# Final projection of a two-layer encoder: five token tiles summed over heads 0 to 5 beside the last head's inversion and recurrence

## What is computed

```
def deltanet_mixer(hn, w_in, conv_w, a_log, dt_bias, out_norm, w_out):
    proj = hn @ w_in                                   # q, k, v, gate, beta, decay
    ...                                                # short conv, silu, l2 norms
    o_fwd = gated_delta_chunked(q, k, v, g[:, :, 0], beta[:, :, 0])
    o_bwd = flip(gated_delta_chunked(flip(q), flip(k), flip(v), ...))
    o = o_fwd + o_bwd
    o = o * lax.rsqrt(jnp.mean(o * o, axis=-1, keepdims=True) + EPS) * out_norm
    o = (o.reshape(b, s, B_VW) * jax.nn.silu(gate)).astype(hn.dtype)
    return o @ w_out                                   # the final projection

x = x + deltanet_mixer(...)                            # residual x1
return rms_norm(x, final_norm)
```

## Time and profile before

| quantity | value |
|---|---|
| median of three executions | 1497.5 us |
| the profiled execution's own time | 1498.05 us |
| its span in the trace | 1496.3 us |
| PE busy | 1378.8 us (92%) |
| PE weight loads busy | 1010.7 us (68%) |
| DVE busy | 785.8 us (53%) |
| ACT busy | 704.0 us (47%) |
| GpSimd busy | 248.8 us (17%) |
| mean granted TensorE clock | 0.961 of full |
| HBM read, written | 61.04 MB, 12.12 MB |

### The profile page before, as it was taken

How to read it: one execution, slowest core, us unless ns; L and a number is a source line. 1 busy time by engine, 2 the same in 40 slices (tenths; PEclk the granted TensorE clock), 3 DMA queues, 4 the chain that set the end, 5 groups by cost and what they waited for, 6 DMA issues and landing times.

```text
span 1496.3 us, 25718 instructions
## 1 busy us (share of the span) xinstructions
PE 1378.8 (92%) x9981; PEld 1010.7 (68%) x9981; DVE 785.8 (53%) x2200; ACT 704.0 (47%) x1869; POOL 248.8 (17%) x190
## 2 busy tenths in 40 slices
PE   5999999999999987799989899999898999977998
PEld 4866666666444456677778778878787787864443
DVE  6244545444344228665665684666655846552232
ACT  6155554555454234363573654644726546462111
POOL 8111111110011313212121221120212211200000
PEclk9999999999999999899999999999999999988999
DMA  5101000011211111010110210101102001015041
GB/s 175 43 28 29 29 28 30 28 57 57 85 57 57 57 73 42 16 43 30 44 43 16 71 29 16 57 29 44 43 16 72 25 21 43 1 55 214 0 141 56
DMA packets 18455, 74.81 MB, mean 50 GB/s; under 512 B 2848, under 2 KB 3104, under 8 KB 16800
## 3 DMA queue, kind: packets, MB, share of 16 engines
q1 hardware_dynamic: 18336, 73.18, 14.3%
HBM read 61.04 MB, written 12.12 MB: 49 GB/s over the span
## 4 chain that ended last, share of the span: by engine, by line
PE 70%; DVE 16%; ACT 7%; issue 3%; DMA 2%; POOL 1%; SPq 0%; DVEq 0%; ACTq 0%; POOLq 0%
PE bank L1570 16%; PE bank L1691 12%; PE bank L1642 8%; PE bank L1671 7%; DVE arena L1314 4%; PE bank L1597 3%; DVE arena L1354 3%; PE bank L1623 3%; PE bank L1608 3%; PE bank L1825 2%; PE bank L1839 2%; PE bank L1842 2%; PE bank L1750 2%; DVE arena L1487 1%; PE bank L1724 1%
## 5 line engine op out<-in xcount | busy, mean ns | idle before, releaser
L1691 PE MATMUL bank<-hn_hi,w_hi 128*128 128x512 f32 x512 | 227.4, 444 | 0.0
L1691 PE MATMUL bank<-hn_hi,w_lo 128*128 128x512 f32 x512 | 206.8, 404 | 0.0
L1691 PE MATMUL bank<-hn_lo,w_hi 128*128 128x512 f32 x512 | 206.0, 402 | 0.0
L1570 PE MATMUL bank<-hn_hi,w_hi 128*128 128x512 f32 x320 | 139.7, 437 | 0.5 <-ACT arena L944 0.2
L1570 PE MATMUL bank<-hn_hi,w_lo 128*128 128x512 f32 x320 | 125.9, 393 | 0.0
L1570 PE MATMUL bank<-hn_lo,w_hi 128*128 128x512 f32 x320 | 125.8, 393 | 0.0
L1671 PE MATMUL bank<-arena 128*128 128x512 f32 x256 | 114.3, 600 | 10.3 <-DMA arena<-oT_scratch 9.1
L1642 PE MATMUL bank<-arena 128*128 128x512 f32 x256 | 120.1, 600 | 0.0
L876 POOL TENSOR_TENSOR w_lo<-arena,w_hi 128x1024 fp32r<-128x1024 f32 x30 | 74.3, 2476 | 266.2 <-ACT w_hi L1038 266.2
L1691 PEld LDWEIGHTS bank<-hn_hi,w_lo 128*128 128x128 f32 x512 | 99.5, 194 | 22.8
L1691 PEld LDWEIGHTS bank<-hn_hi,w_hi 128*128 128x128 f32 x512 | 100.1, 196 | 17.2
(11 more groups left out here) (227 smaller groups left out, 2655.4 us busy)
## 6 DMA issues: line engine op xcount, KB each, us to landing
arena<-in_w SPq DMA_DIRECT2D x52, 512.0 KB, 3.5
arena<-in_x SPq DMA_DIRECT2D x16, 512.0 KB, 4.4
arena<-gc_scratch SPq DMA_DIRECT2D x8, 1024.0 KB, 4.5
x_scratch<-arena SPq DMA_DIRECT2D x8, 512.0 KB, 2.6
arena<-in_wout SPq DMA_DIRECT2D x1, 4096.0 KB, 13.5
arena<-x_scratch SPq DMA_DIRECT2D x8, 512.0 KB, 4.2
out<-arena SPq DMA_DIRECT2D x8, 512.0 KB, 2.9
oT_scratch<-arena SPq DMA_DIRECT2D x7, 512.0 KB, 5.0
```

The costliest lines, as they stand in the source:

```text
L1570: ins = te.matmul(bank[r % 2][:], wp[:, tile % 2, k], hp[:, k, hf * HALF:(hf + 1) * HALF], start=(k == 0 and m == 0), stop=(k == KT - 1 an ...
L1691: ins = te.matmul(b[:], wp[:, t % 2, k], hp[:, k, hf * HALF:(hf + 1) * HALF], start=(k == 0 and m == 0), stop=(k == KT - 1 and m == 2))
```

## The change

The final projection is cut into three parts. `FIN_EARLY` now counts ten units (token tiles 0 to 4), and `FIN_HEADS = 6` heads.

1. Partial sums: for units 0 to 9, heads 0 to 5, 60 matmuls, as events `("fp", u, j)`. They are put by `fe(n)`: 14 in the last inversion behind stage y5, and two behind each of the recurrence's events 1 to 23. They use banks 0 and 1 in turn.
2. A new DVE event `("part", u)` adds the residual tile to each finished partial sum and keeps it in SBUF (`early_sum`, ten halves, in the space of the layer's weight buffers).
3. The rest: events `("ff", w, j)`, in the order of tiles `FIN_TILES = [5, 0, 1, 2, 6, 3, 4, 7]`. For tiles 0 to 4 only heads 6 and 7 are summed, and DVE adds `early_sum` in place of the residual; tiles 5, 6, 7 are done in full. Between osum and otr stand now the 14 matmuls of tile 5.

The loads follow: SP issues them in an event `("finld",)` of the last inversion, as six pairs of DMAs (one head's weight and one head's output, 512 KB each, counted on three semaphores), one of 1 MB for the weight's heads 6 and 7, and then the first two residual tiles. Head 6's output is loaded later, by a DMA of its own. In the diff, `finld` is SP's part, `part` DVE's and `fp` PE's.

```
-FIN_EARLY = 6
+FIN_EARLY = 10
+FIN_HEADS = 6
...
+        FIN_TILES = [5, 0, 1, 2, 6, 3, 4, 7]
...
+            early = [("fp", 2 * u + hf, j) for u in range(1) for j in range(FIN_HEADS) for hf in range(2)]
+            early = [[e] + ([("part", e[1])] if e[2] == FIN_HEADS - 1 else []) for e in early]
+            for u in range(2, FIN_EARLY):
+                early += [[("fp", u, j)] + ([("part", u)] if j == FIN_HEADS - 1 else []) for j in range(FIN_HEADS)]
+            def fe(n):
+                for items in early[:n]:
+                    ev.extend(items)
+                del early[:n]
...
             def inversion(h):
+                more = f if h < B_HEADS - 1 else fe
...
+                if h == B_HEADS - 1:
+                    put(("finld",))
                 stage("x5", h)
...
-                f(3)
+                more(3)
                 put(("vtr", h, 0), ("vtr", h, 1))
                 stage("x6", h)
-                f(2)
+                more(2)
                 stage("y6", h)
-                f(2)
+                more(2)
...
-            fins = [("fin", u, j) for u in range(2) for j in range(B_HEADS - 1)]
             for n in range(3 * NT):
                 put(("rec", h - 1, n // 3, "abc"[n % 3]))
-                if n >= 10 and fins:
-                    put(fins.pop(0))
+                if n >= 1:
+                    fe(2)
...
             put(("osum", h - 1, 0), ("osum", h - 1, 1), ("osq", h - 1))
-            put(*[("fin", u, j) for u in range(2, FIN_EARLY) for j in range(B_HEADS - 1)])
+            put(*[("ff", w, j) for w in range(2) for j in range(KT - 1)])
             put(("onorm", h - 1), ("otr", h - 1, 0), ("otr", h - 1, 1))
+            put(*[("ff", w, KT - 1) for w in range(2)])
+            for w in range(2, 2 * NT):
+                put(*[("ff", w, j) for j in range(FIN_HEADS if 2 * FIN_TILES[w // 2] < FIN_EARLY else 0, KT)])
...
+                elif e[0] == "finld":
+                    sp.wait_ge(W_full, W_DONE[("proj", NTILES - 1, 1, 0)])
+                    sp.wait_ge(st_o, 16 * FIN_HEADS)
+                    for j in range(FIN_HEADS):
+                        sp.dma_start(wout_e[:, j], wout1[:, j]).then_inc(ld_fin[j // 2], 16)
+                        sp.dma_start(oT_e[:, j], oT_d[j]).then_inc(ld_fin[j // 2], 16)
+                    sp.dma_start(wout_e[:, FIN_HEADS:KT], wout1[:, FIN_HEADS:KT]).then_inc(ld_wout1, 16)
+                    sp.wait_ge(conv_done, 3 * B_HEADS)
+                    for j in range(2):
+                        sp.wait_ge(*evicted(("vtr", B_HEADS - 1, j)))
+                    for t in range(2):
+                        sp.dma_start(x1r[:, t], x1_d[:, t, :]).then_inc(ld_x1[t], 16)
...
+                elif e[0] == "part":
+                    u = e[1]
+                    t, hf = u // 2, u % 2
+                    dve.wait_ge(part_full, u + 1)
+                    dve.wait_ge(ld_x1[t % 2], 16 * (t // 2 + 1))
+                    ve.tensor_tensor(early_sum[:, u], bank[u % 2][:], x1r[:, t % 2, hf * HALF:(hf + 1) * HALF], ALU.add).then_inc(part_done, 1)
...
+                elif e[0] == "fp":
+                    u, j = e[1:]
+                    t, hf = u // 2, u % 2
+                    if j == 0:
+                        if u < 2:
+                            pe.wait_ge(*evicted(("proj", NTILES - 1, u, 0)))
+                        else:
+                            pe.wait_ge(part_done, u - 1)
+                    if u == 0 and j % 2 == 0:
+                        pe.wait_ge(ld_fin[j // 2], 64)
+                    ins = te.matmul(bank[u % 2][:], oT_e[:, j, t * P:(t + 1) * P], wout_e[:, j, hf * HALF:(hf + 1) * HALF],
+                                    start=(j == 0), stop=(j == FIN_HEADS - 1))
```

More of the change, by code:

```diff
@@ L216, in hybrid_encoder_kernel @@
         ld_oT = sem("ld_oT")
+        ld_fin = [sem(f"ld_fin{i}") for i in range(FIN_HEADS // 2)]
+        part_full = sem("part_full")
+        part_done = sem("part_done")
         ld_wout = [sem(f"ld_wout0_{i}") for i in range(3)]
@@ L811, in _ @@
+            for n in range(2, NT):
+                sp.wait_ge(fin_y, n + 1)
+                tok = FIN_TILES[n] * P
+                sp.dma_start(out[tok:tok + P, :], ytile[:, n % 2]).then_inc(st_out[n % 2], 16)
             for b in range(2):
@@ L1694, in _ @@
                         ins.then_inc(W_full, 1)
-                elif e[0] == "fin":
-                    fin_sum(e[1], e[2])
+                elif e[0] == "fp":
[4 more added lines that the diff above has]
+                            pe.wait_ge(*evicted(("proj", NTILES - 1, u, 0)))
+                        else:
+                            pe.wait_ge(part_done, u - 1)
[3 more added lines that the diff above has]
+                                    start=(j == 0), stop=(j == FIN_HEADS - 1))
+                    if j == FIN_HEADS - 1:
+                        ins.then_inc(part_full, 1)
+                elif e[0] == "ff":
+                    w, j = e[1:]
+                    t, hf = FIN_TILES[w // 2], w % 2
+                    first = FIN_HEADS if 2 * t < FIN_EARLY else 0
+                    if j == first:
+                        if w < 2:
+                            pe.wait_ge(*evicted(("qtr", B_HEADS - 1, w)))
+                        elif w < 4:
+                            pe.wait_ge(rec_s, B_HEADS * 14)
+                            pe.wait_ge(rec_oa, B_HEADS * O1_ACT)
+                        elif w < 6:
+                            pe.wait_ge(part_done, FIN_EARLY)
+                        else:
+                            pe.wait_ge(fin_add, w - 5)
+                    if w == 0 and j == FIN_HEADS:
+                        pe.wait_ge(ld_wout1, 16)
+                        pe.wait_ge(ld_oT, 16)
+                    if w == 0 and j == KT - 1:
+                        for i in range(2):
+                            pe.wait_ge(*evicted(("otr", B_HEADS - 1, i)))
+                    ins = te.matmul(fin_bank(w)[:], oT_e[:, j, t * P:(t + 1) * P], wout_e[:, j, hf * HALF:(hf + 1) * HALF],
+                                    start=(j == first), stop=(j == KT - 1))
+                    if j == KT - 1:
+                        ins.then_inc(fin_full, 1)
                 elif e[0] == "gtr":
@@ L1872, in _ @@
                                 ins.then_inc(i_y6[p], 1)
-            for u in range(2 * NT):
-                for j in range(KT - 1 if u < FIN_EARLY else 0, KT):
-                    if u == 0 and j == KT - 1:
-                        for i in range(2):
-                            pe.wait_ge(*evicted(("otr", B_HEADS - 1, i)))
-                    ins = fin_sum(u, j)
-                ins.then_inc(fin_full, 1)
 def kernel(**inputs):
```

63 lines of the change are left out of this document (26 added, 37 removed).

## The result

The changed kernel takes 1472.38 us (median of four executions, 1470.44 to 1473.92) against 1497.01 us before (four, 1495.5 to 1498.23): the ratio is 0.9835, 95% interval 0.9822 to 0.9848. That is 24.6 us less. The prediction was 1473.0, with 24.6 us of gain.

A forecast was written before the change was run, and what follows sets the result against it. PE was taken as the bound, with a hole of some 45 us of idle and slow-clock time. From 1334.43, matmuls, stages, transposes and waits sum to 130.3 us, ending PE at 1464.7: 24.6 us gained, 1473 us, range 1470 to 1480.

The forecast's parts named there:

- The step that carried it: From x6's end at 1334.43, PE's work plus few waits sets the end: 130.3 us, so PE ends at 1464.7.
- Loads: Early loads on SP's queue, scaled by bytes: four land at 1326.7, eight at 1331.8, twelve at 1336.9, all at 1339.5.
- The first fourteen: Last inversion: three matmuls fill vtr's 3.17 us gap at no cost; x6's end stays at 1334.43.
- the bound that I had named at 1 us: Last inversion: if the low clock after vtr goes too, x6 ends about 1 us earlier, giving 1472.
- The residual: First addition on DVE: tile 0 lands about 1341, needed at 1342.7; 0.2 us of wait taken, 11.6 if late.
- Rival B: Late loads or residual block DVE's first addition and the recurrence: between 2 and 11.6 us, 1475 to 1484; 12%.
- The recurrence: Recurrence: stages 13.05 us plus 46 matmuls 39.6 us, steps of about 6.9 us, DVE's additions hidden.
- the wait at q's factor: Recurrence step 1: DVE waits for ACT's squares of q's transposes; 0.6 us, between 0 and 1.9.
- Osum, otr, tail: After the recurrence: 14 matmuls (12.0 us) still cover the norm's chain, otr 7 takes 2.19, then 54 tail matmuls.
- rival D: Tail: the gain goes into another limit, DVE's 4.3 us a tile, 35 us against 46.5 on PE; 1%.
- Rival C: Loads run one after another; PE stands 28.6 us, 1501.5 us, slower than before above 3.9 us a transfer; 2%.

The follow-up runs named there:

- e9: The changed kernel itself, unedited, timed once more: 1474.75 us, ratio 0.9845 to the kernel before.
- e6: The changed kernel with every DVE addition of a partial sum and the residual issued twice: 1472.30 us, ratio 0.9835 to the kernel before.
- e7: The changed kernel with token tiles finished in order 0 to 7, leaving 2 matmuls between osum and otr: 1475.12 us, ratio 0.9852 to before.
- e8: The changed kernel with three remaining PE gaps filled (between vtr's halves, at q's factor, at otr's end): 1467.11 us, ratio 0.9799 to before.
- e3: The changed kernel with the recurrence's 46 partial-sum matmuls moved into one piece behind it, ahead of osum: 1485.16 us, ratio 0.9910 to before.
- e5: The changed kernel with SP waiting for each of the twelve 512 KB loads to land before issuing the next: 1496.39 us, ratio 0.9993 to before.
- e1: The kernel before with only the weight and heads 0 to 5 loaded earlier, the 14 recurrence matmuls left in place: 1485.85 us, ratio 0.9915.
- e2: The changed kernel with the last inversion's 14 partial-sum matmuls moved into one piece behind the recurrence: 1477.32 us, ratio 0.9861 to before.

## Why the prediction was right

- **The step that carried it**, "the new end is the sum of PE's work if PE has no waits", held. From the last projection to PE's end it gave 1464.7 - 1318.3 = 146.4 us; measured are 145.4 and, in e9, 147.0. Behind x6's end, where the sum starts, it gave 130.3, and 1461.73 - 1331.12 = 130.6 were measured. By kind of time it came out too: 16.2 of the gain was to be idle time, and 16.0 were.
- **Where luck helped.** The predicted gain, 24.6 us, is exactly that of the medians. But the distance fell by 25.6 us in one trace of the changed kernel and by 24.0 in the other, and a second median of this kernel lay 2.4 us above the first. That the forecast is within a few microseconds is the sum's doing; that it is within one is chance.
- **Loads.** Predicted landings after the last projection were 8.4 us for the fourth load, 13.5 for the eighth, 18.6 for the twelfth and 21.2 for the thirteenth; the changed kernel's trace has 7.6, 14.0, 18.9 and 21.4. Scaling one long transfer by bytes was good to 0.8 us. The first partial sum starts 7.8 us after the projection because y5 ends then, and not because of a load. In e6 the fourth load came after 8.8 us and PE waited 0.99 us for it, and 0.29 in e7, inside the 2 us that vtr's gaps absorb.
- **The first fourteen.** I kept x6's end where it was (16.1 us after the projection). It came at 1331.1, 14.8 us after: the low clock behind vtr was gone in this trace, the bound that I had named at 1 us and which was worth 1.3. In e9 it was not gone.
- **The residual.** 0.2 us were taken, 0 came, but with a margin of half a microsecond only. The tile landed 22.7 us after the last projection, as forecast; it was needed after 23.2 us and not after 24.4, because x6 ended sooner. Rival B's mechanism was close, and e8 shows it at 0.35 us, far below the 2 us at which the rival begins.
- **The recurrence.** Pace 6.95 us predicted, 6.94 measured; the wait at q's factor 0.87 in place of 0.6. The cover is real: e3 loses 11.0 us in the recurrence without it, and e6 shows that DVE's additions cost nothing there.
- **Osum, otr, tail.** 12.0 us for the 14 matmuls between osum and otr, 2.19 and 46.5 predicted; 12.02, 1415.14 - 1412.95 = 2.19 and 46.60 measured. PE has no wait behind otr, so rival D falls.
- **Rival C** had its threshold wrong. I said that the change would turn slower above 3.9 us a transfer; e5 is level with before at 3.5. Three terms were missing. The four matmuls behind the last wait ran at the low clock (6.13 us in place of 3.6). PE was due at head 4 of unit 0 after 20.4 us and not 21.8, so it waited longer. And the residual behind the twelve, which took 5.80 us to land, held PE for another 0.93 us.
- **Where the gain is.** By the distances 12.05 of the 25.6 us come from the early loads alone (e1), and 13.5 from the filling that they make possible. The parts don't add: without the filler in the inversion 5.1 to 6.7 us are lost, without that in the recurrence 11.0, and with the early loads but only the old 14 fillers (e1) 13.5.

## What to carry to other kernels

When a kernel's last stage waits in line behind a latency-bound one, add up the PE work from a fixed point on and look for what else can run in the holes: the gain is at most the idle time plus what the work loses at the low clock. An in-order engine turns every filler whose data is late into a stall of all that stands behind it, so the loads have to be cut in the order in which the filler uses them, and issued without waiting for each other. Take a duration from a row at the clock that the changed kernel will have there.

## What the runs showed of the hardware

- The low clock can last well beyond the idle time in front of it: in e2, behind the gaps of 3.17 and 1.41 us at vtr, the granted clock is 0.50 in each of the five stretches from 1330 to 1340, while PE is busy for 1.65 to 2.00 us of each 2 us. And it depends on more than the program: one kernel shows x6 at 1.15 us in one execution and at 1.98 us in another.
- A DMA of 512 KB alone takes 3.1 to 3.6 us from issue to landing (one took 4.8 in e5). Twelve of them in flight together need 18.9 us in the changed kernel, 1.6 us each.
